# Six weight buffers of a two-layer fp32 kernel: from distances of a multiple of 512 bytes to the input tile to six different distances

## The reference

```python
p = rmsnorm(x) @ w_in                       # first block, 2048 -> 4352
x = x + concat(y_a, y_b, y_c) @ w_out       # 2048 -> 2048
up = dwconv3(rmsnorm(x) @ ffn_w_up, ...)    # 2048 -> 11264
x = x + (silu(gate) * val) @ ffn_w_down     # 5632 -> 2048
proj = rmsnorm(x) @ fox_w_in                # second block, 2048 -> 6160
x = x + rmsnorm(attention(proj) @ fox_w_out)      # 2048 -> 2048
x = x + rmsnorm(square(relu(h @ mlp_w1)) @ mlp_w2)  # 2048 -> 8192 -> 2048
```

## Time and profile before

| | us |
|---|---|
| three runs | 2157.85, 2157.93, 2158.72 |
| the profiled execution's own time | 2158.86 |
| its span (first to last instruction) | 2157.0 |
| TensorE busy in it | 2148.6 |
| VectorE busy | 1303.6 |
| ScalarE busy | 1009.5 |

### The profile page before, as it was taken

How to read it: one execution, slowest core, us unless ns; L and a number is a source line. 1 busy time by engine, 2 the same in 40 slices (tenths; PEclk the granted TensorE clock), 3 DMA queues, 4 the chain that set the end, 5 groups by cost and what they waited for, 6 DMA issues and landing times.

```text
span 2157.0 us, 27987 instructions
## 1 busy us (share of the span) xinstructions
PE 2148.6 (100%) x11694; PEld 1864.5 (86%) x11694; DVE 1303.6 (60%) x1611; ACT 1009.5 (47%) x1186; POOL 64.5 (3%) x85
## 2 busy tenths in 40 slices
PE   9999999999999999999999999999999999999999
PEld 7888888888888888888898889888888888888887
DVE  6868557776777775444655665466555555444445
ACT  6444446545545554444655444455434334444443
POOL 3030000000000000000001010000000000000000
PEclk9999999999999999999999999999999999999999
DMA  9655656566555655555566555546666665555552
GB/s 338 213 172 176 215 183 204 180 196 195 192 184 186 195 181 198 194 194 195 165 205 205 158 176 184 199 144 215 184 189 195 185 188 194 195 195 195 193 190 104
DMA packets 268925, 412.41 MB, mean 191 GB/s; under 512 B 6981, under 2 KB 247045, under 8 KB 250112
## 3 DMA queue, kind: packets, MB, share of 16 engines
q1 hardware_dynamic: 265648, 398.08, 56.6%
q0 software_dynamic: 2432, 11.75, 1.5%
q10 hardware_dynamic: 720, 0.79, 0.1%
HBM read 408.49 MB, written 2.11 MB: 190 GB/s over the span
## 4 chain that ended last, share of the span: by engine, by line
PE 97%; DMA 1%; DVE 1%; ACT 1%; SPq 0%; issue 0%; ACTq 0%; DVEq 0%
PE bank L1546 35%; PE bank L1559 18%; PE bank L1607 11%; PE bank L1608 11%; PE bank L1612 11%; PE bank L1549 2%; PE bank L1561 2%; PE bank L1550 2%; DMA M<-in_xt 1%; PE bank L1441 1%; PE bank L1398 0%; DMA X<-in_x 0%; DVE M L1304 0%; PE bank L1524 0%; PE bank L1491 0%; PE bank L1477 0%
## 5 line engine op out<-in xcount | busy, mean ns | idle before, releaser
L800 DVE TENSOR_TENSOR wlo<-raw,whi 128x2048 fp32r<-128x2048 f32 (+1 forms) x372 | 852.5, 2293 | 760.5 <-ACT whi L480 760.4
L480 ACT ACTIVATE whi<-raw 128x2048 fp32r<-128x2048 f32 (+1 forms) x371 | 710.3, 1916 | 781.5 <-PE bank L1612 421.3
L1546 PE MATMUL bank<-hh,whi 128*128 128x512 f32 x3360 | 807.2, 392 | 0.6 <-ACT whi L480 0.6
L1546 PEld LDWEIGHTS bank<-hh,whi 128*128 128x128 f32 x3360 | 618.3, 188 | 123.5 <-ACT whi L480 1.0
L1559 PEld LDWEIGHTS bank<-hh,wlo 128*128 128x128 f32 x3360 | 430.7, 191 | 16.3
L1559 PE MATMUL bank<-hh,wlo 128*128 128x256 f32 x3360 | 436.0, 283 | 0.0
L1607 PE MATMUL bank<-whi,hh 128*128 128x512 f32 x1072 | 417.6, 390 | 0.0
L1608 PE MATMUL bank<-whi,hh 128*128 128x512 f32 x1072 | 417.1, 389 | 0.0
L1612 PE MATMUL bank<-wlo,hh 128*128 128x512 f32 x1072 | 264.8, 389 | 0.0
L1607 PEld LDWEIGHTS bank<-whi,hh 128*128 128x128 f32 x1072 | 201.2, 188 | 41.9 <-DVE M L868 0.2
L1612 PEld LDWEIGHTS bank<-wlo,hh 128*128 128x128 f32 x1072 | 201.2, 188 | 41.8
(11 more groups left out here) (247 smaller groups left out, 941.8 us busy)
## 6 DMA issues: line engine op xcount, KB each, us to landing
raw<-in_mlp_w SPq DMA_DIRECT2D x128, 1024.0 KB, 5.5
raw<-in_ffn_w_up SPq DMA_DIRECT2D x88, 1024.0 KB, 5.1
raw<-in_ffn_w_down SPq DMA_DIRECT2D x44, 1024.0 KB, 4.8
raw<-in_fox_w_in SPq DMA_DIRECT2D x32, 1024.0 KB, 5.4
raw<-in_w_in SPq DMA_DIRECT2D x31, 1024.0 KB, 5.5
raw<-in_fox_w_in SPq DMA_DIRECT2D x16, 1032.0 KB, 5.4
raw<-in_w_out SPq DMA_DIRECT2D x16, 1024.0 KB, 4.8
raw<-in_fox_w_out SPq DMA_DIRECT2D x16, 1024.0 KB, 4.8
```

Of the source, the lines that this page charges most:

```text
L480: e.activation(whi[i % RING][:, 0:n], raw[i % RAW][:, 0:n], ACT.Copy).then_inc(s_hi, 1)
L800: e.tensor_tensor(wlo[i % RING][:, 0:n], raw[i % RAW][:, 0:n], whi[i % RING][:, 0:n].bitcast(F), ALU.subtract).then_inc(s_lo, 1)
L1546: e.matmul(bank[b][:, :], wh[:, k, s], hh[:, kk, :], start=kk == 0, stop=False)
```

## The change

The order of the tiles in SBUF is another, and the unused tiles between them are smaller. No instruction is added, removed or moved on any engine; operands differ by their addresses alone. `hh`, `X`, `ident`, `ones` and `M` keep their distances from one another; the six buffers of split weights, the four of raw weights, `st`, `edge`, `cols` and `rb` get new ones. `cols` has 516 words, so the unused tile of 8 words ahead of `wlo1` brings what follows back to a multiple of 64 bytes. Unused tiles took 2240 bytes a partition and take 160.

```diff
-        def gap(i, words):
-            sb(f"gap{i}", [P, words])
-
-
-        st = sb("st", [P, 80])
-        raw = [sb("raw0", [P, UN])]
-        whi, wlo = [], []
-        for i in range(RING):
-            whi.append(sb(f"whi{i}", [P, UN], R))
-            raw.append(sb(f"raw{i + 1}", [P, UN]))
-            gap(2 * i, 96)
-            wlo.append(sb(f"wlo{i}", [P, UN], R))
-            if i == 0:
-                edge = sb("edge", [P, 64])
-            gap(2 * i + 1, 48 if i == 0 else 112)
-        hh = sb("hh", [P, KD, 2 * T], R)
+
+        tiles = {}
+        for name, before, shape, dt in (
+                ("rb", 0, [P, T], F),
+                ("raw1", 0, [P, UN], F),
+                ("wlo2", 0, [P, UN], R),
+                ("wlo0", 0, [P, UN], R),
+                ("whi1", 0, [P, UN], R),
+                ("whi2", 16, [P, UN], R),
+                ("whi0", 16, [P, UN], R),
+                ("edge", 0, [P, 64], F),
+                ("raw0", 0, [P, UN], F),
+                ("cols", 0, [P, NCOL], F),
+                ("raw2", 0, [P, UN], F),
+                ("wlo1", 8, [P, UN], R),
+                ("raw3", 0, [P, UN], F),
+                ("st", 0, [P, 80], F),
+                ("hh", 0, [P, KD, 2 * T], R)):
+            if before:
+                sb(f"before_{name}", [P, before])
+            tiles[name] = sb(name, shape, dt)
+        st, edge, rb, cols, hh = (tiles[n] for n in ("st", "edge", "rb", "cols", "hh"))
+        raw = [tiles[f"raw{i}"] for i in range(RAW)]
+        whi, wlo = ([tiles[f"{n}{i}"] for i in range(RING)] for n in ("whi", "wlo"))
...
         M = sb("M", [P, 18496])
-        cols = sb("cols", [P, NCOL])
         ones = onesr[:, :].bitcast(F)
-        rb = sb("rb", [P, T])
```

## The result

The changed kernel takes **2171.19 us**, median of 3 runs (2171.13 to 2172.46), against 2157.93 before: ratio 1.0062, 95% interval 1.0047 to 1.0076. It is slower by 13.3 us. I forecast 2150 and 0.42 for faster; the range 2112 to 2190 holds the time, the sign is wrong.

The account below looks back on a forecast made before the run. TensorE's matmul steps were taken to bound the kernel: span 2157.0 less 8.2 us for the split buffers, nothing for unit starts and other tiles, gave 2148.8, adjusted to a median run of 2150 us; range 2112 to 2190.

Parts of the forecast that it names:

- The frame: Whole kernel: TensorE's start-to-start steps sum to the time; placement acts only through them or by making TensorE wait.
- edit 1: Six split-weight buffers moved off multiples of 512 bytes: 0.8 ns less on each of 10,224 matmuls, 8.2 us less.
- the extra: Time each 256- or 512-column matmul takes beyond its columns: 13.3 ns, over 10,224 matmuls 136 us, 6% of the kernel.
- rival A: 512-column matmuls: zero distance is good, off zero steps never settle; about 5 ns each, 33 us slower, 2191 us; chance 0.31.
- Edit 2: Starts of units in flow "w" and `rows`: dear beginnings could spread (+4 us) or go (-4.7 us); set at nothing.
- Edit 3: Other tiles (`raw`, `cols`, `rb`, `st`, `edge`), read by splits and small vector work: set at nothing, any slowing covered.
- its case of half the buffers: 512-column matmuls: the never-settling loss holds for half of the buffers only, 16 us slower, 2174 us.
- Rival B: All matmuls: distance matters only below 64 bytes, so no change, 2158 us; chance 0.26.
- Rival C: All matmuls: extra is mostly a zero-distance clash; 6 ns less for two thirds, 41 us less, 2117 us; chance 0.14.

Follow-up runs that it names:

- The experiment that missed by 21 us: Low parts of the split weights all at distance 64, high parts at 0, otherwise the kernel before the change: 2159.42 us, ratio 1.0007 to that kernel.

## Why the prediction was wrong, point by point

**The frame held.** Nothing waits, the step of TensorE is all that changed, and the distance moves it both ways by several ns. The bounds of edit 1 were -6 and +8 ns, and the settled steps that the runs found lie from 6.7 ns less (256 columns at 64) to 7.6 more (512 columns at 96). That the range held the time is no merit of the mean in it.

**The step that failed is edit 1, "off zero, on the mean of several relations, the extra is 0.8 ns less. I take that: 10,224 x 0.8 ns".** It carried a value of matmuls of 258 columns over to 6576 matmuls of 512. It also counted all 10,224 as touched, though `wlo0` at 256 reads as 0. Measured, on the mean of all: -2.9 ns for 256 columns, so the proxy had the sign right for its own width and was too small, and +3.6 ns for 512. The sum over both is +13.1 us where -8.2 stood. The row that spoke of 512 columns was there, the 396 ns of the first matmul of a unit beside 389, and I kept it for rival A alone. With signs by width, 6576 x +3.5 (the middle of 0 and 7) less 3648 x 0.8 gives some +20 us. The sign would have been right, but the size by luck: those 396 ns were read at distance 0.

**Edit 2**, beginnings of units, nothing, +-4.7 us: the dear beginnings of flow "w" went. A high run of before takes 27 ns more than 16 settled steps; in the change the three high runs take 4 and 5 ns more and 3 less than 16 of their own settled steps (233.3, 233.3 and 228.9). That is some 5 us less, at the low end of the bounds, and it is part of the sums above: the settled 512-column steps of flow "w" alone cost some 17 us. What a beginning costs depends on what stood before (the high run at 0 takes 3648, 3699 or 3663 ns behind 160, 192 or 224).

**Edit 3**, the other tiles, nothing: right. VectorE and ScalarE are busy for 1304.2 and 1009.6 us where they were for 1303.6 and 1009.5, and TensorE has no idle time to speak of before its matmuls.

**Rival A**, slower: right in its sign and, at 512 columns, near in size (+3.6 of its 5 ns; its case of half the buffers gave 2174 us); its reason, that off zero the steps never settle, was not: they settle, on another value. It left out what the 256-column matmuls give back, 10.6 us. **Rival B**, only distances below 64 count: falls, 64 alone costs 23.9 us in the high parts. The rule of the Trainium skill beside it, page "SBUF — State Buffer", section "Who interferes with whom", that TensorE waits on no one, would make this 0; here the distance of TensorE's own load from its own stream is worth 1.1% of the kernel. **Rival C**, much faster: the 6 ns are real (113.3 against 120 ns, 256 columns at 64 behind a high part at 64), but none of the distances tried at 512 columns has a settled step below the 226.7 of distance 0.

## What to carry to other kernels

In a loop in which each matmul brings its own fp32 weight load, the place of the loaded slice relative to the streamed one was a knob worth 3% of a step of 512 columns and 6% of one of 256 here, with different best values for the two: try it per shape and per stage, not for the kernel as a whole. A proxy from another shape is worth little; where the kernel holds even one row of the shape that dominates, price by that. And where stages want different places, tiles that are some words longer (56 here) give each its own without an instruction more: here 7.3 us, a ratio of 0.9963. The experiment that missed by 21 us had taken the step of a distance from behind one high run to behind another: measure the high and the low run together, not one of them.

## What the runs showed that I had not expected

**The period is 256 bytes, and the relation is mirrored.** The change has 64 and 320 in two high buffers, and their runs are 3737 and 3738 ns; 256 reads as 0 (1895 ns for the low run behind a high part at 64, with `wlo0` at 256 in the change and at 0 in the kernel with the high parts at 64). In flow "w" the weights from the buffers are loaded and `hh` streams, in `rows` it is the other way round. A high part at 64 settles at 233.3 ns in flow "w" and at 228.9 in `rows`, one at 192 at 228.9 and at 233.3. So a distance d on one side is about -d on the other; it is not exact, since 128, its own mirror image, has 232.4 ns in flow "w" and 233.3 in `rows`.

| distance of the loaded slice, flow "w" | 16 of 512 columns, ns | 16 of 256 columns, ns |
|---|---|---|
| 0 | 3654 | 1913 (1895 behind a high part at 64) |
| 16, 48 | | 1893, 1893 |
| 32 | 3733 | 1897 |
| 64 | 3737 (3728 with all at 64) | 1887 (1818 behind a high part at 64) |
| 96 | 3746 | 1880 |
| 112 | | 1916 |
| 128 | 3716 | 1895 |
| 160 | | 1921 |
| 192 | 3659 | 1884 |
| 224 | | 1865 |

These are sums of exact steps in the traces of the runs above. The empty cells were not tried. The low runs at 32, 96 and 128 stand behind high parts at the same distance, that at 192 behind one at 0 (1885 behind one at 192), the others without a note behind high parts at 0.

**A step has a memory.** The same 256-column matmuls at 64 take 113.3 ns each behind a high run at 64 and 117.7 behind one at 0, from the second of the 16 to the last, and in nearly all units: with low parts alone at 64, 201 of the 210 low runs take 1885 to 1890 ns, with all at 64, 192 take 1818 to 1829. What is carried over I could not tell.

**The settled means of four cases lie on a raster.** Before, the settled steps are 226.7 and 120.0 ns; at other distances 233.3 and 113.3. These are multiples of 6.67 ns (34, 18, 35 and 17), the time of 16 columns at 2.4 GHz. The single steps are not: at 64 they are 236 and 231 ns by turns. The values between are means over patterns that repeat, as 226, 229 and 232 ns for 228.9; at 96 the pattern has seven steps and a mean of 234.3. The 13.3 ns of extra that the prediction started from are two units of 6.67. What makes them, no run here shows.
